# Transposes of attention probabilities placed inside the weight units

## The reference

```python
def hybrid_layer(x, gain, w_in, f_bias, w_branch, w_out):
    h = rms_norm(x, gain)
    proj = jnp.einsum('bsd,de->bse', h, w_in)
    (qa, ka, va, ga, qb, kb_, vb_, gb, qc, kc, vc, gc,
     q_idx, k_idx, w_idx, f_logit, merge_logit) = jnp.split(proj, SPLIT_POINTS, axis=-1)
    oa = moba_attention(...) * jax.nn.silu(ga)        # causal softmax, 8 heads of 64
    ob = dsa_attention(...) * jax.nn.silu(gb)         # causal softmax over the 64 best keys of an index
    oc = forgetting_attention(...) * jax.nn.silu(gc)  # causal softmax with a running bias
    y = jnp.einsum('nbsw,nwd->bsnd', jnp.stack([oa, ob, oc], axis=0), w_branch)
    gates = jax.nn.sigmoid(merge_logit).reshape(B, S, N_BRANCH, D_MODEL)
    merged = jnp.sum(gates * y, axis=2)
    return x + jnp.einsum('bsd,de->bse', merged, w_out)
```

## Time and profile before

| what | value |
|---|---|
| median of 3 runs | 1585.98 us |
| lowest and highest of them | 1585.73, 1588.92 us |
| span of the profiled execution | 1587.3 us |
| TensorE, matmuls (PE) | 1542.8 us busy, 97% |
| VectorE (DVE) | 1040.1 us, 66% |
| ScalarE (ACT) | 754.6 us, 48% |
| the chain that ended last | PE 77%, DVE 8%, issue 8%, ACT 5% |

### The profile page before, as it was taken

The page is one execution under the profiler, slowest core; times in us unless marked ns, Lnnn a source line. Parts: engine busy times, 40 slices in busy tenths (PEclk is TensorE's granted clock), DMA queues, the critical chain, the costliest instruction groups (busy, mean ns, idle before and its releaser), DMA issues.

```text
span 1587.3 us, 31432 instructions
## 1 busy us (share of the span) xinstructions
PE 1542.8 (97%) x13599; PEld 1475.0 (93%) x13599; DVE 1040.1 (66%) x1347; ACT 754.6 (48%) x1132; POOL 97.5 (6%) x79
## 2 busy tenths in 40 slices
PE   5999999999999999999999999999999999989999
PEld 5998999999998999999999999999999996889999
DVE  4878766577877665655456667977345447767674
ACT  4555554455455554554446331333245426655453
POOL 0311000002110000000010000000010102000000
PEclk9999999999999999989999999999999999999999
DMA  7676544566775546512134647764235424255754
GB/s 254 218 242 217 166 160 159 163 221 223 243 230 175 171 151 208 188 54 97 37 107 133 205 150 248 234 213 143 74 100 175 118 81 96 74 151 153 232 170 136
DMA packets 312333, 260.92 MB, mean 164 GB/s; under 512 B 24066, under 2 KB 298498, under 8 KB 312068
## 3 DMA queue, kind: packets, MB, share of 16 engines
q1 hardware_dynamic: 294260, 253.52, 50.1%
q10 hardware_dynamic: 17936, 5.40, 1.6%
HBM read 257.85 MB, written 1.05 MB: 163 GB/s over the span
## 4 chain that ended last, share of the span: by engine, by line
PE 77%; DVE 8%; issue 8%; ACT 5%; DMA 1%; POOL 0%; SPq 0%; DVEq 0%; ACTq 0%; POOLq 0%
PE banks_g L1411 34%; PE banks_g L948 21%; PE banks_g L1121 5%; PE banks_g L938 4%; PE banks_g L1270 2%; DVE w_lo L2190 2%; PE banks_g L971 1%; PE bank_s L1069 1%; ACT probs L1748 1%; ACT w_hi L1588 1%; PE bank_o L1096 1%; PE banks_g L930 1%; PE bank_t L1082 1%; DVE w_lo L2488 1%; DVE probs L2385 1%
## 5 line engine op out<-in xcount | busy, mean ns | idle before, releaser
L1411 PE MATMUL banks_g<-h_hi,w_lo 128*128 128x256 f32 x1296 | 360.5, 278 | 1.0 <-DVE w_lo L2488 0.6
L1411 PE MATMUL banks_g<-h_lo,w_hi 128*128 128x256 f32 x1296 | 358.5, 277 | 0.0
L1411 PE MATMUL banks_g<-h_hi,w_hi 128*128 128x256 f32 x1296 | 358.5, 277 | 0.0
L2488 DVE TENSOR_TENSOR w_lo<-raw,w_hi 128x2048 fp32r<-128x2048 f32 (+1 forms) x100 | 208.2, 2084 | 99.7 <-ACT w_hi L1784 99.6
L2190 DVE TENSOR_TENSOR w_lo<-raw,w_hi 128x2048 fp32r<-128x2048 f32 x92 | 212.5, 2311 | 68.3 <-ACT w_hi L1588 67.7
L1411 PEld LDWEIGHTS banks_g<-h_hi,w_lo 128*128 128x128 f32 x1296 | 243.9, 188 | 3.0 <-issue 0.9
L1411 PEld LDWEIGHTS banks_g<-h_lo,w_hi 128*128 128x128 f32 x1296 | 243.3, 188 | 0.1
L1411 PEld LDWEIGHTS banks_g<-h_hi,w_hi 128*128 128x128 f32 x1296 | 243.3, 188 | 0.0
L948 PE MATMUL banks_g<-h_hi,w_lo 128*128 128x256 f32 x800 | 225.8, 282 | 0.7 <-DVE w_lo L2190 0.7
L948 PE MATMUL banks_g<-h_hi,w_hi 128*128 128x256 f32 x800 | 221.9, 277 | 0.0
L948 PE MATMUL banks_g<-h_lo,w_hi 128*128 128x256 f32 x800 | 221.9, 277 | 0.0
(11 more groups left out here) (414 smaller groups left out, 3275.8 us busy)
## 6 DMA issues: line engine op xcount, KB each, us to landing
raw<-w_in SPq DMA_DIRECT2D x76, 1024.0 KB, 5.0
raw<-w_up SPq DMA_DIRECT2D x88, 512.0 KB, 5.1
ada_raw<-ada_w SPq DMA_DIRECT2D x24, 1024.0 KB, 7.1
raw<-w_down SPq DMA_DIRECT2D x32, 704.0 KB, 4.4
raw<-w_branch SPq DMA_DIRECT2D x12, 1024.0 KB, 4.9
ada_raw<-ada_t SPq DMA_DIRECT2D x12, 1024.0 KB, 4.9
late_raw<-ada_t SPq DMA_DIRECT2D x12, 1024.0 KB, 5.0
raw<-qkv SPq DMA_DIRECT2D x12, 1024.0 KB, 4.9
```

Source lines behind the costliest of these rows:

```text
L1411: last = nc.tensor.matmul(to, w[:, c, m0:m0 + P], a[:, c, s_ * SEQ:s_ * SEQ + SEQ], start=(m, s_, c, n) == (0, 0, 0, 0), stop=(m, s_, c, n ...
L2488: nc.vector.tensor_tensor(w_lo[:, u % SLOTS, 0:n], raw[:, u % SLOTS, 0:n], w_hi[:, u % SLOTS, 0:n].bitcast(F32), ALU.subtract).then_inc(dv ...
```

## The change

The `turn` entries leave the order. Instead, TensorE runs the transposes of batch k inside weight unit 2k+6: those of the first 128 keys ahead of its step 3 (after 9 of the 48 matmuls), and for qt = 1 those of the second 128 keys ahead of its step 9 (after 27). ScalarE copies the first out ahead of its weight split `high(u+2)` of that unit, and the second behind it, ahead of emptying the unit's bank. The waits and the instructions themselves stay as they are.

```diff
+TURNS = {2 * k + 6: k for k in range(4, len(BATCHES))}
+TURN_AT = (3, 9)
...
         order.append(("unit", kind, i))
-        k = (n - 6) // 2
-        if n % 2 == 0 and 4 <= k < len(BATCHES) and BATCHES[k][1]:
-            order.append(("turn", k, 1))
...
                 order.append(("o low", k - 1))
-            if 4 <= k < len(BATCHES):
-                order.append(("turn", k, 0))
...
+            def turn(k, kt):
+
+                pe.wait_ge(dve_steps, dve_.at(f"probs{k}"))
+
+                if (k, kt) == (4, 0):
+                    pe.wait_ge(act_steps, act_.at(f"turned15 {BATCHES[15][1]}", before=True))
+                else:
+                    pk, pt = (k, 0) if kt else (k - 1, BATCHES[k - 1][1])
+                    pe.wait_ge(act_steps, act_.at(f"turned{pk} {pt}"))
+                for s in range(4):
+                    last = nc.tensor.transpose(bank_t[:, s, :], probs[k % 2][:, s, kt * P:kt * P + P], ident[:, :])
+                last.then_inc(pe_steps, pe_.step(f"turn{k} {kt}"))
+
+            def turn_inside(u, done):
+
+                if u in TURNS and done in TURN_AT[0:BATCHES[TURNS[u]][1] + 1]:
+                    turn(TURNS[u], TURN_AT.index(done))
...
                                     for c in range(KC):
+                                        turn_inside(u, t * KC + c)
...
                                         m0 = j * 256 + m * P
+                                        turn_inside(u, j * 2 * kcs + 2 * c + m)
...
-                    elif what == "turn":
-                        k, kt = arg
-                        pe.wait_ge(dve_steps, dve_.at(f"probs{k}"))
...
+                def turned_out(k, kt):
+
+                    act.wait_ge(pe_steps, pe_.at(f"turn{k} {kt}"))
+                    nc.scalar.activation(probs_t[:, kt, :, :], bank_t[:, :, :], ACT.Copy
+                                         ).then_inc(act_steps, act_.step(f"turned{k} {kt}"))
...
                         kind, i = arg
+                        if u in TURNS:
+                            turned_out(TURNS[u], 0)
                         if u + AHEAD < len(UNITS):
                             high(u + AHEAD)
+                        if u in TURNS and BATCHES[TURNS[u]][1]:
+                            turned_out(TURNS[u], 1)
...
-                    elif what == "turn":
-                        k, kt = arg
-
-                        act.wait_ge(pe_steps, pe_.at(f"turn{k} {kt}"))
-                        nc.scalar.activation(probs_t[:, kt, :, :], bank_t[:, :, :], ACT.Copy
-                                             ).then_inc(act_steps, act_.step(f"turned{k} {kt}"))
```

## The result

The changed kernel takes 1579.41 us (median of 4 runs, 1578.58 to 1581.81) against 1586.2 us of the kernel before (median of 4 runs). The medians differ by 6.8 us. The ratio on record is 0.9947, its 95% interval 0.9933 to 0.9962; it isn't the ratio of these two medians, and of 1586.2 us it makes 8.4 us less, with 6.0 and 10.6 as the ends. Forecast were 1578.0 us and 8.0 us less.

A forecast was written before the change was run, and what follows sets the result against it. TensorE, busy 97% of the span, was taken to bound the kernel, so only holes in its matmul stream count. 5.3 + 4.0 - 2.0 + 0.7 = 8.0 us off 1585.98 gave 1578.0 us, range 1574.5 to 1582.6.

The forecast's parts named there:

- The waits of transposes, 5.3 us: TensorE's eight waits for VectorE's normalised probabilities before transposes vanish, covered by nine matmuls: 5.3 us gained.
- The waits before `values`, 4.0 us: TensorE's four open waits for ScalarE's copy of transposed probabilities before `values` go: 4.0 us gained.
- What comes back, 2.0 us: Batches 7 and 15: TensorE comes earlier, VectorE's probabilities do not; 0.5 us each, 2.0 us lost over two layers.
- The pitch, 0.7 us: Weight units behind delayed turns: half of eight become quick, 5.48 instead of 5.66 us; 0.7 us gained, bounds -1.5 and +1.5.
- The interruption costs nothing: Transposes inside a weight unit cost TensorE what they cost between units: 0 taken, 3.6 us at worst for 36 turns.
- ScalarE's later split, cost 0 and "just covered": Weight split up to 1.05 us later behind the first copy; VectorE's w_lo still done before the next mask: cost 0.
- Waits that all come back deeper: VectorE's chain from mask to probabilities paces two units, so TensorE meets it later: 1.6 us gained, 1584.4; chance 0.10.
- ScalarE too late for the second transposes: One transpose bank: inside the unit the second transposes wait for the first copy; batch 7 has 0.7 us spare; chance 0.03.
- More than counted: Batches 7 and 15 do not wait and all eight units become quick: 10.7 us gained, 1575.3; chance 0.10.
- The clock: TensorE's clock falls to 1.2 GHz, doubling a unit's 5.5 us; one unit a layer costs 11 us, 1589; chance 0.01.

The follow-up runs named there:

- e4: Changed kernel, but ScalarE copies the second transposes out behind the emptying of the unit's bank, as before the change; ratio 0.9959 to the kernel before.
- e3: Changed kernel with its transposes at steps 6 and 12 in place of 3 and 9; ratio 0.9931 to the kernel before.
- e9: Changed kernel with transposes at steps 6 and 12, and ScalarE splitting before the first copy in branch units; 1575.48 us, ratio 0.9912 to the kernel before.
- e5: Changed kernel, but ScalarE makes the weight split first, then copies out first and second transposes; ratio 0.9966 to the kernel before.
- e7: Kernel before, transposes between units, but VectorE normalises only the first 8 keys of each head (output no longer the attention); ratio 0.9953 to the kernel before.
- e1: Changed kernel with only the first transposes inside the unit, the second and their copy behind it as before; ratio 0.9954 to the kernel before.
- e2: Changed kernel with only the second transposes inside the unit, the first between units as before; ratio 0.9989 to the kernel before.
- e6: Changed kernel with the rope of set b's keys after unit 18 in place of unit 17; ratio 0.9938 to the kernel before.

## Why the prediction was right, and where it was off

**The waits of transposes, 5.3 us: right.** In its old form the wait is gone everywhere; the four that are left are new ones, deeper in the unit. **The waits before `values`, 4.0 us: right**, and e4 shows the cause that was named: the copy's place in ScalarE's queue. The weight-load figures were the ones to use: by them, and 4.5 ns for each slow pitch, the sum closes to 0.3 us in every kernel of the table. Before, 9.2 us; changed, 3.6; the difference of 5.6 and 3.0 us of pitch (336 x 4.5 ns in each layer) make 8.6 of the 8.8 measured.

**What comes back, 2.0 us: mis-sized, it measured 3.6.** The places were right, batches 7 and 15, and so was the reason, VectorE's chain. For batch 7 the probabilities came when the prediction said: it had them release the transposes at 164.94, 51.23 us behind the start of scores 4 (113.71), and in the changed kernel that is 112.96 and 164.19, again 51.23. The wait was 0.92 us instead of 0.5, because TensorE was there earlier than was worked out. For batch 15 it was 0.81 instead of 0.5: 0.15 us because VectorE's way from normalisation 14 to mask 15 grew from 10.16 to 10.31 us, the rest TensorE again. What brought TensorE there too early is mostly the next term (two units ahead of batch 7 and one ahead of batch 15 ran 0.18 us quicker each in layer 0).

**The pitch, 0.7 us: mis-sized, it measured 3.0.** The rows shown had 5.66 us behind a delayed turn and 5.48 behind a punctual one, and the prediction looked for slow units only behind delayed turns. Of the four such units of a layer three became quick and the fourth in part, while unit 20, with batch 7's new wait inside, became partly slow: 1.1 us in two layers. But five more units of each layer ran slow with no delayed turn ahead of them (19, or 29 in layer 1, and 22 to 25), and all five became quick but for a few pitches: 1.9 us. So not everything that the change could take away stood in the lines of waits. The two errors, -1.6 and +2.3 us, nearly cancel. In part they must, since a TensorE that is earlier at VectorE's late result waits longer; that the rest cancels is luck, and the forecast of 8.0 us is nearer to the measured 8.8 than its terms are to theirs.

**The interruption costs nothing: right.** In all the rows of the trace a punctual turn inside the unit starts 0.12 us after the matmul before it and the next weight matmul 0.03 us after its last start, as between units. The sum above leaves at most 0.3 us for the 36 turns, with either sign.

**ScalarE's later split, cost 0 and "just covered": right for this change, but with no margin.** In the changed kernel a w_lo waited 0.29 us for it ahead of mask 15 (L2200 at 263.56). Three steps deeper it was 1.2 us, and the cover was gone (e3); e9 took the delay away and with it the last wait.

**The rivals.** Waits that all come back deeper: those of two batches a layer, no more. ScalarE too late for the second transposes: not with this order, by e5's with the other. The margin worked out for batch 7 was 0.7 us; with 1.9 us more in front of the copy that leaves a wait of 1.2 us, and e5 has 0.9 (a gap of 1.03 less the usual 0.12), which is near it. More than counted: batches 7 and 15 did wait, so this rival's condition failed, though the units it wanted quick became so, and others with them. The clock: 1.00 in both stretches in all ten kernels. The Trainium skill, TensorE: Matmul & The Clock Gate, Part 4, says that transposes do not count as busy for the gate; no run here shows a lower clock for four or eight of them among 48 matmuls.

Open stays why a unit settles on a pitch of 113 or 118 ns. Behind a turn it shows in the first few matmuls and is mostly kept. Of all turns with weight matmuls behind them, in the ten kernels, 44 were delayed by 0.3 us or more, and behind 42 of these the matmuls ran slow; 280 were punctual or nearly so, and behind 16 of these they did. 12 of the 16 are the turns of batches 8 and 9, ahead of units 22 and 24, in the three kernels with `turn k 0` between the units. So a delay goes with the slow pitch, and e7 shows the delay's removal to remove it; for units 22 to 25 it goes with the place of the first transposes, as e1 and e2 show. Why is not shown. Nor is a turn needed: unit 37, which has none right ahead of it or inside, runs slow in e2, e3, e6 and e9 and quick in the others, in both layers.

## What to carry to other kernels

In a stream that one engine bounds, look whether a small step that needs another engine's late result can stand some way inside the next long block instead of at its edge. Every matmul in front of it is cover, and the rest of the block covers the copy.

Count then what else moves with it in the other engine's in-order queue. Here the first copy had to go ahead of the weight split, or the second transposes waited for it (e5). But the split that it holds back may itself be missed next (e3), and the best of the ten kernels came only when depth and order were changed together (e9).

And what the consumer gains ahead of a late result comes back as a wait, unless the producer's own chain starts earlier too.

## What the hardware showed beside

- The weight matmuls here (128x256, float32) ran at one of two pitches, 113 to 114 ns or 117 to 118 ns, at the same granted clock of 1.00. Behind a delayed turn the first gap is mostly 200 to 201 ns and most gaps after it 117 to 119; behind a punctual one it is mostly 206 to 207, then 118, and 113 from there. Over a unit that is about 0.2 us, and the change took 3 us of it out of the two layers.
- Four transposes of 128x128 amid such matmuls cost 0.45 us, inside an open accumulation of another bank as well as between two units.
- The stretch of 173 to 179 us repeats from layer to layer to 0.02 us, in one execution, in eight of the ten kernels (0.10 us in e4, 0.30 in e5), while whole executions of one kernel differ by 3 to 7 us. For changes of this size the stretch in the trace was the sharper measure, and it ordered all kernels as the times did but for e6 and the changed kernel, and e1 and e7, whose times are within each other's intervals.
